# The order of the gate products, the one-hot rows and the pick repeats in a retrieval kernel

## What is computed

```
s1, i1 = top_k(s[:, :, 0], 16);  s2, i2 = top_k(s[:, :, 1], 16)      # keys 0..127 in each half
sc, pos = top_k(s1[.., :, None] + s2[.., None, :], 16)               # 8 heads x 16 picks per token
eidx = i1 * 128 + i2 at pos;  gate = softmax(sc)                     # 128 experts of 16384 per token
act = gelu(x . u_tab[eidx]);  y = (gate * act) . v_tab[eidx]
```

## Time and profile before

| | us |
|---|---|
| median of three runs | 3354.37 |
| the profiled execution, its own time | 3355.55 |
| its span | 3353.7 |
| TensorE (PE) busy | 3152.7, 94% |
| VectorE (DVE) busy | 2303.5, 69% |
| ScalarE (ACT) busy | 1625.5, 48% |

### The profile page before, as it was taken

One profiled execution on the slowest core, in us unless ns is written; L12 is line 12 of the kernel. 1 busy time (PEld: TensorE's weight loads), 2 busy tenths in 40 slices (PEclk: granted clock), 3 DMA queues, 4 the chain that ended last, 5 costly groups with the idle time before them and its releaser, 6 DMA issues.

```text
span 3353.7 us, 71932 instructions
## 1 busy us (share of the span) xinstructions
PE 3152.7 (94%) x25820; PEld 2792.3 (83%) x25820; DVE 2303.5 (69%) x5029; ACT 1625.5 (48%) x2325; POOL 159.3 (5%) x102
## 2 busy tenths in 40 slices
PE   8999998799999999987999989999889999879998
PEld 4899997488888999965888889887789999658887
DVE  6578876877765888667666675555458886775555
ACT  6544445744454444466544455232344444664454
POOL 0000000000000000000000056111100000000000
PEclk9999999999999999999999999999899999999999
DMA  8445552077765555512676734000245554125664
GB/s 329 164 166 183 176 171 95 26 250 238 243 231 169 185 181 178 170 64 78 237 262 237 251 111 154 15 3 3 85 147 184 182 178 164 45 89 197 202 193 133
DMA packets 144461, 533.89 MB, mean 159 GB/s; under 512 B 16752, under 2 KB 16912, under 8 KB 142016
## 3 DMA queue, kind: packets, MB, share of 16 engines
q1 hardware_dynamic: 141120, 514.01, 45.6%
q0 software_dynamic: 3200, 17.85, 1.5%
HBM read 525.50 MB, written 6.30 MB: 159 GB/s over the span
## 4 chain that ended last, share of the span: by engine, by line
PE 86%; DVE 5%; ACT 4%; issue 3%; POOL 1%; DMA 1%; SPq 0%; DVEq 0%; ACTq 0%; POOLq 0%
PE pS L1857 12%; PE pS L1859 12%; PE pS L1858 12%; PE pY L1976 10%; PE pY L1980 10%; PE pY L1978 10%; PE pY L2055 3%; ACT raw L634 3%; PE pG L1951 2%; PE pS L1951 2%; PE pY L1940 2%; PE pS L2055 2%; PE pG L2055 1%; POOL lo L1731 1%; PE pY L1890 1%
## 5 line engine op out<-in xcount | busy, mean ns | idle before, releaser
L1050 DVE TENSOR_TENSOR lo<-raw,hi 128x1024 fp32r<-128x1024 f32 x824 | 1009.4, 1225 | 634.5 <-ACT hi L582 631.1
L582 ACT CAST hi<-raw 128x1024 fp32r<-128x1024 f32 x872 | 913.6, 1048 | 527.6 <-PE pY L1980 508.5
L1857 PE MATMUL pS<-h_hi,hi 128*128 128x256 f32 x3552 | 1014.4, 286 | 21.1 <-DVE h_lo L1640 9.0
L1858 PE MATMUL pS<-h_lo,hi 128*128 128x256 f32 x3552 | 1006.3, 283 | 0.0
L1859 PE MATMUL pS<-h_hi,lo 128*128 128x256 f32 x3552 | 1006.2, 283 | 0.0
L1857 PEld LDWEIGHTS pS<-h_hi,hi 128*128 128x128 f32 x3552 | 682.8, 192 | 36.6 <-issue 32.7
L1858 PEld LDWEIGHTS pS<-h_lo,hi 128*128 128x128 f32 x3552 | 683.0, 192 | 0.2
L1859 PEld LDWEIGHTS pS<-h_hi,lo 128*128 128x128 f32 x3552 | 682.8, 192 | 0.0
L1976 PE MATMUL pY<-hi,h_hi 128*128 128x512 f32 x1536 | 475.4, 391 | 11.0 <-DVE h_lo L1219 11.0
L1978 PE MATMUL pY<-lo,h_hi 128*128 128x512 f32 x1536 | 474.4, 390 | 0.0
L1980 PE MATMUL pY<-hi,h_lo 128*128 128x512 f32 x1536 | 474.3, 390 | 0.0
(11 more groups left out here) (319 smaller groups left out, 3227.2 us busy)
## 6 DMA issues: line engine op xcount, KB each, us to landing
raw<-in_blocks SPq DMA_DIRECT2D x872, 512.0 KB, 3.3
g<-in_mod_tiles SPq DMA_DIRECT2D x56, 512.0 KB, 4.7
raw<-in_mod_wT SPq DMA_DIRECT2D x20, 512.0 KB, 8.4
buf<-in_mod_wT SPq DMA_DIRECT2D x20, 512.0 KB, 8.2
buf<-in_keysT POOLq DMA_DIRECT2D x3, 1024.0 KB, 5.2
buf<-in_window SPq DMA_DIRECT2D x2, 1024.0 KB, 11.2
spill_x_res<-buf POOLq DMA_DIRECT2D x2, 1024.0 KB, 4.7
spill_x_h<-buf POOLq DMA_DIRECT2D x2, 1024.0 KB, 7.2
```

The source lines that it names most:

```text
L582: s.copy(hi[slot][:, :, :], raw[slot][:, :, :]).then_inc(hi_ready, 1)
L1050: v.tensor_tensor(lo[slot][:, :, :], raw[slot][:, :, :], hi[slot][:, :, :].bitcast(F32), ALU.subtract).then_inc(lo_ready, 1)
L1857: t_.matmul(out, hi[slot][:, c, :], h_hi[:, c, :], start=(c == 0), stop=False)
L1858: t_.matmul(out, hi[slot][:, c, :], h_lo[:, c, :], start=False, stop=False)
```

## The change

- `gate_octet` takes a range of tokens, `row_products` a list of units. TensorE's order in an octet becomes: gates of tokens 0 to 4, the q = 2 rows of the next octet, gates of tokens 5 to 7, the q = 0 and 1 rows of the octet after that. Ahead of the first octet, the q = 2 rows of octet 0 come behind the last u block.
- `hots` is laid out as 32 rows in a line, so that one-hot(i2) and part q = 2 of tokens 4 to 7 are 12 rows side by side. One comparison makes all 12 (`gate_hots`), and one multiplication by a bfloat16 gate then scales the last 4 (`gate_part3`); these two replace the comparison and the four one-token instructions. VectorE's order becomes: comparison of o+2, apply(o), multiplication of o+2.
- The pick columns for it are written as pairs (`pick_pairs`, `part3_pairs`) in `g4`, and the code table moves to `gT`. So GpSimd issues the second load of the code table behind `mod_ready` 5 rather than behind the last use of a `mod_tile`.
- The repeats come four at a time, ahead of every fourth u block, and the four stand on four different strips (`span_at`); `span_rows` of the first two of four follow one `split_lo`, those of the third and fourth the next two.
- `U_PICKS` becomes 100, and the eight `off_a` steps stand one a block.

```diff
-        hots = [halves(raw_flat[:, 2 * D:4 * D], 4, OCTET, P), halves(raw_flat[:, 0:2 * D], 4, OCTET, P)]
+        hots = [halves(raw_flat[:, 2 * D:4 * D], 4 * OCTET, P), halves(raw_flat[:, 0:2 * D], 4 * OCTET, P)]
...
+        HOT2, ROWS3, ROWS = 0, OCTET, 2 * OCTET
+        def row_of(q, t):
+            return ROWS + OCTET * q + t if q < 2 else ROWS3 + (t + QUAD) % OCTET
+        def span_at(n):
+            i = n if n < N_SPAN else n - N_SPAN
+            return i // BITS, 2 * (i % QUAD) + i % BITS // QUAD
...
-        U_PICKS = 96
+        U_PICKS = NE - RING - N_SPAN - N_HALF
...
                 def gate_hots(o):
+                    n = OCTET + QUAD
                     if o >= 2:
                         ve.wait_ge(gates_mm, N_OCT * g + o - 1)
-                    v.tensor_tensor(hots[o % 2][:, 0].rearrange("p t (a b) -> p t a b", b=2),
-                                    iota_b[:, :].rearrange("p (a b) -> p a b", b=2).unsqueeze(1).to_broadcast([P, OCTET, P // 2, 2]),
-                                    i2p[:, OCTET * o:OCTET * (o + 1), :].unsqueeze(2).to_broadcast([P, OCTET, P // 2, 2]), ALU.is_equal)
-                    for t in range(QUAD):
-                        c = QUAD * o + t
-                        i = v.tensor_scalar(hots[o % 2][:, 3, QUAD + t, :], iota_b[:, :], i1_cols[:, c:c + 1], g3_cols[:, c:c + 1],
-                                            ALU.is_equal, ALU.mult)
-                    i.then_inc(onehot, 1)
+                    v.tensor_tensor(hots[o % 2][:, HOT2:HOT2 + n].rearrange("p t (a b) -> p t a b", b=2),
+                                    iota_b[:, :].rearrange("p (a b) -> p a b", b=2).unsqueeze(1).to_broadcast([P, n, P // 2, 2]),
+                                    pick_pairs[:, o].unsqueeze(2).to_broadcast([P, n, P // 2, 2]), ALU.is_equal).then_inc(compared, 1)
+                def gate_part3(o):
+                    x = hots[o % 2][:, ROWS3:ROWS3 + QUAD].rearrange("p t (a b) -> p t a b", b=2)
+                    ve.wait_ge(compared, N_OCT * g + o + 1)
+                    v.tensor_tensor(x, x, part3_pairs[:, o].unsqueeze(2).to_broadcast([P, QUAD, P // 2, 2]), ALU.mult).then_inc(onehot, 1)
...
                 for i in range(N_SPAN + N_HALF):
                     split_lo(None, ku + U_PICKS, i + AHEAD)
-                    span_rows(i)
+                    if i % QUAD == 0:
+                        span_rows(i)
+                    if i % QUAD < QUAD - 1:
+                        span_rows(i + 1)
...
                 for o in range(N_OCT):
+                    if o + 2 < N_OCT:
+                        gate_hots(o + 2)
                     apply_gates(o)
                     if o + 2 < N_OCT:
-                        gate_hots(o + 2)
+                        gate_part3(o + 2)
...
-            pool.wait_ge(mod_tile_used, MOD_TILES[0])
+            pool.wait_ge(mod_ready, 5)
             gate_tables()
...
+                def span_quad(n0):
+                    if n0:
+                        pe.wait_ge(spans_made, (N_SPAN + N_HALF) * g + n0)
+                    for r in range(1 if n0 < N_SPAN else NT):
+                        for n in range(n0, n0 + QUAD):
+                            at, c = span_at(n)
+                            q, par = c // 2, c % 2
+                            strip = slice(2 * SPAN * q, 2 * SPAN * (q + 1))
...
                 for j in range(RING - 1):
                     u_block(NE - RING + j)
                 pe.wait_ge(spans_made, (N_SPAN + N_HALF) * (g + 1))
-                row_products(0)
+                row_products(0, (0, 1))
                 u_block(NE - 1)
-                row_products(1)
+                row_products(0, (2,))
+                row_products(1, (0, 1))
                 for o in range(N_OCT):
                     if o == 1:
                         pe.wait_ge(evacuated, 2 + e0 + NQ + NE)
-                    gate_octet(o)
+                    gate_octet(o, range(0, 5))
+                    if o + 1 < N_OCT:
+                        row_products(o + 1, (2,))
+                    gate_octet(o, range(5, OCTET))
                     if o + 2 < N_OCT:
-                        row_products(o + 2)
+                        row_products(o + 2, (0, 1))
```

More of the change, by code:

```diff
@@ L351, in build @@
         spans3 = halves(g4_all[:, 0:4 * P], N_HALF, P)
-        i2p = halves(g4_all[:, 4 * P:6 * P], T, 2)
-        code = halves(g4_all[:, 6 * P:8 * P], 4 * P)
-        i1_cols, g3_cols = gT[:, 0:P], gT[:, P:2 * P]
+        pick_pairs = halves(g4_all[:, 4 * P:7 * P], N_OCT, OCTET + QUAD, 2)
+        part3_pairs = halves(g4_all[:, 7 * P:8 * P], N_OCT, QUAD, 2)
+        code = gT[:, :].bitcast(BF16)
         picks_x = halves(flat[:, 122 * T:124 * T], NT, 4 * P)
@@ L1149, in gate_columns @@
                     ve.wait_ge(picksT, g + 1)
[L1150 to L1153, removed]
+                    octets = lambda x: x.rearrange("p (o t) -> p o t", t=OCTET)
+                    pairs = lambda x: x.unsqueeze(3).to_broadcast([P, N_OCT, x.shape[2], 2])
@@ L1315, in parts_b @@
                     v.tensor_copy(part(0), by_tile(gate3)).then_inc(picks_ready, 1)
[L1317 to L1322, removed]
+                return ([softmax_in] + [off_a(m) for m in range(1, TAIL + 1)] +
                         [gather(which, tile, hs, part) for which in range(2) for tile in range(NT) for hs in range(2) for part in range(3)] +
@@ L1899, in peer @@
                 mm.then_inc(picksT, 1)
[L1901 to L1915, removed]
+                def span_quad(n0):
[6 more added lines that the diff above has]
+                            strip = slice(2 * SPAN * q, 2 * SPAN * (q + 1))
+                            if n < N_SPAN:
+                                mm = t_.matmul(pY[:, n % RING, 0:3 * P], repeat_all[strip, 0, par, :], picks_x[strip, at, P:4 * P],
+                                               start=True, stop=True, skip_group_check=True)
+                            else:
+                                mm = t_.matmul(pY[:, n % RING, 0:2 * P], repeat_all[strip, 1 + r, par, :], picks_x[strip, r, 0:2 * P],
+                                               start=(r == 0), stop=(r == NT - 1), skip_group_check=True)
+                            if n0 < N_SPAN or r == NT - 1:
+                                mm.then_inc(spans_mm, 1)
                 def u_block(b):
@@ L1921, in peer, with row_products @@
                 for i in range(N_SPAN + N_HALF):
[L1922 to L1924 removed]
+                    if i % QUAD == 0:
+                        span_quad(i)
                     u_block(U_PICKS + i)
[L1926 to L1929 removed]
+                def row_products(o, units):
                     i = o // 2
[L1932 removed]
+                    for q in units:
                         u = 3 * o + q
@@ L1941, in row_products, with gate_octet @@
                         mm.then_inc(rows_mm, 1)
[L1943 to L1949, removed]
+                def gate_octet(o, tokens):
+                    if tokens[0] == 0:
+                        pe.wait_ge(onehot, N_OCT * g + o + 1)
+                        pe.wait_ge(rows_made, 3 * (N_OCT * g + o) + 3)
+                        if o >= 2:
+                            pe.wait_ge(gated, N_OCT * g + o - 1)
+                    for t in tokens:
                         for q in range(3):
-                            mm = t_.matmul(bank_pair[o % 2][:, t // QUAD, (t % QUAD) * P:(t % QUAD + 1) * P], hots[o % 2][:, 0, t, :],
-                                           hots[o % 2][:, 1 + q, t, :], start=(q == 0), stop=(q == 2), skip_group_check=True)
-                    mm.then_inc(gates_mm, 1)
+                            mm = t_.matmul(bank_pair[o % 2][:, t // QUAD, (t % QUAD) * P:(t % QUAD + 1) * P], hots[o % 2][:, HOT2 + t, :],
+                                           hots[o % 2][:, row_of(q, t), :], start=(q == 0), stop=(q == 2), skip_group_check=True)
+                    if tokens[-1] == OCTET - 1:
+                        mm.then_inc(gates_mm, 1)
                 for j in range(RING - 1):
```

15 lines of the change are left out of this document (9 added, 6 removed).

## The result

The changed kernel takes 3269.65 us (median of 4 runs, 3263.93 to 3270.61) for 3353.69 before in the same runs: a ratio of 0.9748, 95% interval 0.9731 to 0.9765. The forecast was 3276, so the gain of 84 us is some 5 larger than the 79 forecast. The profiled execution after took 3269.11 and its span is 3267.3.

A forecast was written before the change was run, and what follows sets the result against it. A chain of waits between TensorE and ScalarE was taken to pace the gating, TensorE's work the repeats. 3355.55 - 64.5 (gating) - 14.5 (repeats) = 3276.5, median taken as 3276 us, range 3260 to 3294.

The forecast's parts named there:

- part 1: Gating, TensorE's order in an octet: period falls from 3.34 to 2.58 us, third activation late every second octet.
- (a): Gating: TensorE's work alone sets the period, 2.41 us, 15 us more gain, 3261 us; chance 0.1.
- (b): Gating: ScalarE's chain stretches the period to 2.72 us, 12 us less gain, 3288 us; chance 0.19.
- (e): Gating: ScalarE's activations each take some 0.14 us longer, the wait only moves, period 3.0, 3311 us; chance 0.05.
- part 2: Gating on VectorE: comparison 0.95 us, product 0.41; work per octet falls from 2.71 to 2.35, below the 2.58 period.
- Rival (c): Gating: VectorE becomes the bound, comparison and product at the float32 rate, period 3.43 us, 3351 us; chance 0.02.
- part 3: Gating stage's start and end: start loses 0.7 us, end gains 0.2; a stage gains 21.5, three stages 64.5.
- Rival (d): Gating: TensorE's clock falls to 0.50, period 4.6 us; with all three stages low 3453 us; chance 0.02.
- Two of the signs: Changed profile's gating stage: ScalarE's busy share at 90% or more, and the stage near 88 us for 110.
- The wait of the gates for `onehot`: Gating: TensorE's gates waiting for VectorE's `onehot` would show the forecast wrong; the wait was held to be covered.
- part 4: Repeats ahead of the gating, four at a time: 15.2 us in three steps, 14.5 taken; 11.7 if two run at once.
- part 5: Moved blocks, single `off_a` steps, pick columns, code table: nothing for all; under 1 us if hidden cover were gone.

The follow-up runs named there:

- e9_old_vector: e4_start with VectorE's gating as before the change: comparison of 8 rows and four one-token instructions, behind the apply; 3261.35 us.
- e4_start: The changed kernel with ScalarE's activation of octet 0's q = 2 rows moved behind the copy of v block 1 and the last Gelu; 3256.88 us.
- e1_two_offs: The changed kernel with the eight `off_a` steps two a block again; 3275.15 us.
- e5_four_products: e4_start with the product of part q = 2 done by four VectorE instructions of 128 elements, not one of 512; 3258.24 us.

## Why the prediction came out right

**The order on TensorE** (part 1) held to the hundredth: 5.16 for two octets, with the wait of every second q = 1 group for the third activation as the main thing late. The turns cost 0.10 and 0.09 each as read. Rivals (a), (b) and (e) fall with it: ScalarE's activations take 1.02 and 0.60 us on the mean in all three stages, as before. The cut at 4 shows the first activation as the other limit of the chain.

**VectorE** (part 2): 0.96 and 0.42, below the chain as worked out; another order or four products for one change nothing, the full old form costs 4 us. Rival (c) falls. The old sum of 2.71 was 0.09 too high, for the same reason as in e9_old_vector.

**The start** (part 3) was seen as the one place that pays, and its chain was right: q = 2 of octet 1 started 7.92 us after the first rows (555.34 - 547.42), for 8.04 forecast. What the sum lacked is the clock. It fell at that point, in or just behind the second of two waits of TensorE at the start (0.68 and 1.92 us), and the third rows came 9.53 after the first and not 8.96. From there to the last gate the three stages took 80.9, 82.7 and 81.1 us for the 29 x 2.58 + 4.48 = 79.3 of the forecast; e4_start, at a clock of 1.00, took 79.1. So a stage gained 19.1, 17.4 and 18.9 and not 21.5, 9 us less in all. Rival (d) had a true core, but it priced the low clock for whole stages and not for the 7 to 10 us behind the start, and its cause is the waits that the change brought there. Two of the signs missed for the same reason: ScalarE is busy for 88% of the stage (79.5 of 90.6) and not 90%, and a stage is 90 to 92 us and not 88. The wait of the gates for `onehot`, named as a sign of being wrong, shows only in the last octet of a stage, 0.9 us in two waits.

In return the v blocks started at 1.00, where the earlier trace rows show 0.50. The v stages were 5 us shorter together, though 3 us of that are one long stage (355.5, step 2 before). In it TensorE's loads stood 2.4 us in the middle of the v blocks and 1.2 near their start, for 1.6 and 1.1 after. In the middle they waited for VectorE, which stood behind the load of a modulation tile, 3.4 us before and 2.7 after; why the wait for that load differs is not shown. The rows are of before:

```profile
1700.38 1.22 DVE L1211 SCALAR_TENSOR_TENSOR g<-g,gated 128x1024 f32<-128x1024 f32 x1 [3.43 <-DMA g<-in_mod_tiles]
...
1702.00 0.30 PEld L1976 LDWEIGHTS pY<-hi,h_hi 128*128 128x128 f32 x2 [2.38 <-DVE h_lo L1219]
```

**The repeats** (part 4): 14.5 taken, 15 found, and the 11.7 that the prediction gave for two repeats at a time is what quads on two strips gave, 11.5.

**The index steps** (part 5) were set at nothing, and this was wrong. The double steps held VectorE for 3.6 us in blocks of 2.88, and singling them gives 2.5 a step, 7.6 in all. The row stood in the list of waits that was read:

```profile
PE pS L1857 <- DVE lo L1050: 6.6, 12, 0.7
```

I took "under full TensorE" from the stretch of the repeats, for a stretch that I had not looked at.

The forecast gain of 79 stands beside 86 in the traces. The mechanism of the two main parts was right, but that the total came so near is luck: two errors, 9 too much for the stage, since the clock was left out, and 7.6 too little for the index steps, nearly cancel, and the v and delta parts add 9 that was not forecast.

## What to carry to other kernels

When every engine of a stage is partly idle, write the period as a sum of starts along one chain, and then write the new chain with the same rows; here that gave the new period to 0.01 us. Work moved behind a block takes everything queued behind its consumer with it: the start was priced at 0.7 us a stage and cost 4.5 to 6.1 us against e4_start, and one activation moved on ScalarE gave 12.8 us. And a term set at nothing for cover needs the row of its own stretch.

## What the runs showed of the hardware

- Four matmuls of 32 contraction rows and 384 columns on four strips start within 0.01 us and take 0.34 together, as one does; two and two on the same strip take 0.50. A quad with an increment of a semaphore on each of the four cost 0.47, for 0.45 worked out without any term for increments.
- Behind waits of 0.68 and 1.92 us with 15 matmuls between them the granted clock stood at 0.50 in all 12 stages that have both, though TensorE was busy for 5.66 of the 6 us from 555 on. With the wait of 0.68 alone it stayed at 1.00 in all 15. How long it stayed low differs: 6.9, 10.2 and 6.8 us in the three stages of the changed kernel, 3.4, 3.4 and 6.9 in e1_two_offs, where the gating is the same. No run has the wait of 1.92 alone.
- On VectorE a bfloat16 product of 128 elements starts 0.14 us after the one before (four of them span 0.62 in e5_four_products), a one-token compare-and-multiply with two column scalars 0.22 (0.97 for four in e9_old_vector).
